# Squares for the first RMS sum added on VectorE instead of TensorE, and the first adaptive weights asked for one tile of x earlier

## The reference

```python
def rms_norm(x, g):
    xf = x.astype(jnp.float32)
    y = xf * lax.rsqrt(jnp.mean(xf * xf, axis=-1, keepdims=True) + EPS)
    return (y * g.astype(jnp.float32)).astype(x.dtype)
...
    cond = jax.nn.silu(c)
    for l in range(DEPTH):
        mod = cond @ w_ada[l] + b_ada[l]
        shift1, scale1, gate1, shift2, scale2, gate2 = [m[:, None, :] for m in jnp.split(mod, 6, axis=-1)]
        h = rms_norm(x, norm1_g[l]) * (1.0 + scale1) + shift1
        p_lru, p_sb, p_gdn, p_rw = _split(h @ w_in[l], MIXER_IN)
        ...  # four mixers, their gates and branches, w_out, a second norm, ConvFFN, a last norm
```

## Time and profile before

| | us |
|---|---|
| median of 3 runs | 1926.4 |
| the 3 runs | 1924.95 to 1929.25 |
| the profiled execution | 1924.12 |
| its span (first to last instruction) | 1922.3 |
| PE busy | 1873.8 (97%) |
| DVE busy | 935.1 |
| POOL busy | 919.5 |
| ACT busy | 456.5 |

### The profile page before, as it was taken

One profiled execution on the slowest core, in us unless ns is written; L12 is line 12 of the kernel. 1 busy time (PEld: TensorE's weight loads), 2 busy tenths in 40 slices (PEclk: granted clock), 3 DMA queues, 4 the chain that ended last, 5 costly groups with the idle time before them and its releaser, 6 DMA issues.

```text
span 1922.3 us, 33848 instructions
## 1 busy us (share of the span) xinstructions
PE 1873.8 (97%) x14266; PEld 1499.6 (78%) x14266; DVE 935.1 (49%) x1449; ACT 456.5 (24%) x715; POOL 919.5 (48%) x1100
## 2 busy tenths in 40 slices
PE   6999999999999999999999999999999999999997
PEld 4778777767787887887887787888888888888885
DVE  4856578754546546545545826432233322323326
ACT  4441344351222212213213413210110101101103
POOL 2777656523233223223324574455565555646655
PEclk9999999999999999999999999999999999999999
DMA  8516211232212122122135631111111111111112
GB/s 329 215 42 232 97 56 66 88 137 68 72 57 80 65 69 78 47 88 78 41 106 187 219 98 33 33 55 44 55 44 44 55 44 55 44 54 44 46 52 88
DMA packets 72025, 163.52 MB, mean 85 GB/s; under 512 B 6112, under 2 KB 30816, under 8 KB 71904
## 3 DMA queue, kind: packets, MB, share of 16 engines
q1 hardware_dynamic: 64416, 142.88, 22.2%
q10 hardware_dynamic: 7488, 18.88, 2.6%
HBM read 133.17 MB, written 28.57 MB: 84 GB/s over the span
## 4 chain that ended last, share of the span: by engine, by line
PE 83%; DVE 8%; issue 3%; POOL 2%; ACT 2%; DMA 1%; SPq 1%; DVEq 0%; ACTq 0%; POOLq 0%
PE gbank L639 55%; PE mbank L1215 11%; PE mbank L964 3%; PE gbank L1111 1%; POOL w_lo L533 1%; DVE state L2179 1%; DVE fa L1929 1%; POOL w_hi L529 1%; PE gbank L964 1%; PE mbank L720 1%; PE mbank L887 1%; PE gbank L741 1%; PE gbank L1170 1%; DVE fa L1856 1%; DVE h_lo L2308 1%
## 5 line engine op out<-in xcount | busy, mean ns | idle before, releaser
L529 POOL TENSOR_TENSOR w_hi<-w_raw,zero 128x256 fp32r<-128x256 f32 (+1 forms) x508 | 387.2, 792 | 930.9 <-PE gbank L639 767.6
L639 PE MATMUL gbank<-h_hi,w_hi 128*128 128x512 f32 x1648 | 657.7, 399 | 1.0 <-POOL w_lo L533 1.0
L639 PE MATMUL gbank<-h_lo,w_hi 128*128 128x512 f32 x1648 | 648.2, 393 | 0.0
L639 PE MATMUL gbank<-h_hi,w_lo 128*128 128x512 f32 x1648 | 647.9, 393 | 0.0
L533 POOL TENSOR_TENSOR w_lo<-w_raw,w_hi 128x256 fp32r<-128x256 f32 (+1 forms) x508 | 459.0, 934 | 10.0
L639 PEld LDWEIGHTS gbank<-h_hi,w_hi 128*128 128x128 f32 x1648 | 309.4, 188 | 79.1 <-issue 14.5
L639 PEld LDWEIGHTS gbank<-h_hi,w_lo 128*128 128x128 f32 x1648 | 309.4, 188 | 66.9 <-issue 1.5
L639 PEld LDWEIGHTS gbank<-h_lo,w_hi 128*128 128x128 f32 x1648 | 309.6, 188 | 65.4 <-issue 2.9
L1215 PE MATMUL mbank<-ra,w_hi 128*128 128x512 f32 x640 | 197.0, 389 | 0.0
L1215 PEld LDWEIGHTS mbank<-ra,w_hi 128*128 128x128 f32 x640 | 120.1, 188 | 24.9
L2355 DVE SCALAR_TENSOR_TENSOR fa<-mbank,mod,fa 128x1024 f32<-128x1024 f32 x40 | 51.4, 1284 | 169.2 <-PE mbank L1215 169.2
(11 more groups left out here) (355 smaller groups left out, 2196.7 us busy)
## 6 DMA issues: line engine op xcount, KB each, us to landing
w_raw<-in_w_tail SPq DMA_DIRECT2D x74, 512.0 KB, 3.7
fa<-in_w_ada SPq DMA_DIRECT2D x48, 512.0 KB, 6.0
w_raw<-in_w_in SPq DMA_DIRECT2D x26, 512.0 KB, 4.3
p_scr<-fa ACTq DMA_DIRECT2D x20, 512.0 KB, 2.7
w_raw<-in_w_mix SPq DMA_DIRECT2D x16, 640.0 KB, 4.0
fa<-in_xT SPq DMA_DIRECT2D x16, 512.0 KB, 7.9
w_raw<-in_w_gate SPq DMA_DIRECT2D x16, 512.0 KB, 4.0
sig_scr<-fa ACTq DMA_DIRECT2D x32, 256.0 KB, 2.0
```

Of the source, the lines that this page charges most:

```text
L529: last = pool.tensor_tensor(hi[:, c], raw[:, c], zero[:, 0:1].to_broadcast([P, w]), ALU.add)
L639: mm = pe.matmul(gb[bank], w, r, start=(q == 0), stop=(q == 3 * ks - 1))
```

## The change

Four edits belong together.

DVE adds the squares of x1 to x6 (six additions, not three). PE sums over features only the tile of those seven squares (`fa[:, 9]`) and that of x7 (`fa[:, 10]`): 4 multiplies, 8 instructions, not 20, and the first of them now waits for the sixth addition. `sq_used` counts the two finished halves. ACT's squares of x6 and x7 wait for DVE (`x_sq`) where they waited for PE, and its first logarithm waits for the first half alone. SP waits for x5, not for x6, before it asks for the adaptive weights.

```diff
@@ SP
-            sp.wait_ge(sem("x_in6"), 16)
+            sp.wait_ge(sem("x_in5"), 16)
             for t in range(16):
@@ PE
             pe.wait_ge(sem("ones_in"), 16)
-            for k in range(3, KT):
-                if k == 3:
-                    pe.wait_ge(sem("x_sq"), 3)
-                else:
-                    pe.wait_ge(sem("sq"), k + 1)
-                for hf in range(2):
-                    last = pe.matmul(mb[hf], m_("ones"), fa[:, 9 if k == 3 else 8 + 2 * (k % 2), hf * HALF:(hf + 1) * HALF],
-                                     start=(k == 3), stop=(k == KT - 1))
-                last.then_inc(sem("sq_used"), 1)
+
+            pe.wait_ge(sem("x_sq"), KT - 2)
+            for hf in range(2):
+                pe.matmul(mb[hf], m_("ones"), fa[:, 9, hf * HALF:(hf + 1) * HALF], start=True, stop=False)
+            pe.wait_ge(sem("sq"), KT)
+            for hf in range(2):
+                pe.matmul(mb[hf], m_("ones"), fa[:, 10, hf * HALF:(hf + 1) * HALF], start=False, stop=True).then_inc(sem("sq_used"), 1)
@@ ACT
             for k in range(KT):
                 act.wait_ge(sem(f"x_in{k}"), 16)
-                if 3 <= k < 6:
+                if k >= 3:
                     act.wait_ge(sem("x_sq"), k - 2)
-                elif k >= 6:
-                    act.wait_ge(sem("sq_used"), k - 4)
                 act.activation(fa[:, 8 + 2 * (k % 2) if k else 9, :], fa[:, k, :], ACT.Square).then_inc(sem("sq"), 1)
 
             act.preload_act_table_set("natural_log_exp_and_others")
-            act.wait_ge(sem("sq_used"), KT - 3)
             act.wait_ge(sem("zero_set"), 5)
             for hf in range(2):
+                act.wait_ge(sem("sq_used"), hf + 1)
                 act.activation(fa[:, 9, hf * HALF:(hf + 1) * HALF], mb[hf], ACT.Ln, bias=eps[:, 0:1],
                                scale=1.0 / D).then_inc(sem("ln1"), 1)
@@ DVE
-            for k in range(1, 4):
+            for k in range(1, KT - 1):
                 dve.wait_ge(sem("sq"), k + 1)
                 if k >= 2:
                     dve.wait_ge(sem("x_sq"), k - 1)
                 dve.tensor_tensor(fa[:, 9, :], fa[:, 9, :], fa[:, 8 + 2 * (k % 2), :], ALU.add).then_inc(sem("x_sq"), 1)
@@ DVE, mod_in
                 if part == 0:
-                    dve.wait_ge(sem("sq_used"), KT - 3)
+                    dve.wait_ge(sem("sq_used"), 2)
```

## The result

The changed kernel takes **1929.43 us** (median of 20 runs, 1927.66 to 1931.43) against 1926.39 for the kernel before, run on the same chips (20 runs, 1923.69 to 1929.64): ratio **1.0016**, 95% interval 1.001 to 1.0022. It is slower by 3.0 us, clear of the noise, but by less than the 0.2% that the prediction named as the line. The forecast was 1930.2, with a range of 1927.9 to 1932.3. One of the changed kernel's own executions was profiled; its span is 1928.4 us.

A forecast was written before the change was run, and what follows sets the result against it. PE is busy 97% of the span; at the start the later of transfer and norm paths binds. Norm path +4.2 us puts the first product 3.8 later: 1926.4 becomes 1930.2 us, range 1927.9 to 1932.3.

The forecast's parts named there:

- the 0.2%: Smallest difference from no change this kernel's measurement can tell, 3.9 us; the forecast 3.8 lies at that line.
- What bounds: At the start, transfer path (32.6 us, binding) and norm path (32.15) end within 0.5 us; the later sets PE's first product.
- The additions: DVE's additions and POOL's whole passes take turns: new ones about 3.2, 2.8 and 3.3 us, the sixth ending at 24.0.
- the first rival: DVE's additions do not wait for POOL's whole passes, ending at 19.4 to 19.7; faster by about 0.7, 1925.7 us; chance 0.07.
- The sum on PE: PE's eight sum instructions start cold at 24.15 us; the last starts at 28.9, 4.2 later than before.
- no rise in the sum: PE's clock stays low through all eight sum instructions: last start at 30.2, 5.5 us later than before.
- I take 4.2, the row of the same instructions: Choice for PE's sum: clock rises 3.3 us after the first multiply, as before; alternatives gave 3.8 and 5.5.
- What follows the sum: Part 0, h_norm and low part move along; the ask is hidden; first product at 36.4, 3.8 us later.
- The clock at the products: PE's first products begin at half clock, costing 1.3 us before; the forecast left this unchanged.
- the slow stretch: PE's clock at 0.51 between 31.8 and 35.2 us, 2.6 us of it on products, cost 1.3.
- the second rival: Clock stays full at the first products since part 1 is dense and later: −1.3, 1928.9 us; chance 0.27.
- The total: Whole kernel: +3.8 us on the median 1926.4 gives 1930.2; forecast's own chance 0.44.

The follow-up runs named there:

- ask_only: The kernel before with only the earlier ask (SP waits for x5, not x6): 1925.17 us, ratio to before 1.0001.
- pieces_late: The changed kernel with POOL's first split in pieces of 256 columns and SP's ask put back behind x6: 1925.8 us, ratio to before 1.0005.
- pieces: The changed kernel with POOL's first split in pieces of 256 columns instead of whole tiles of 1024: 1923.31 us, ratio to before 0.999.
- defer: The changed kernel with POOL's first split begun only after the sixth addition: 1924.41 us, ratio to before 0.9992.
- adds_only: The changed kernel with SP's ask put back behind x6, so only additions and sum differ from before: 1929.36 us, ratio to before 1.0024.
- warm: The changed kernel with 17 multiplies, results unread, keeping PE busy ahead of the sum: 1926.96 us, ratio to before 1.0012.
- before_pieces: The kernel before with only POOL's first split in pieces of 256 columns: 1925.32 us, ratio to before 1.0001.
- pieces_warm: The changed kernel with POOL's first split in pieces of 256 columns and 12 unread multiplies ahead of PE's sum: 1922.48 us, ratio to before 0.9984.

## Why the prediction came out right, point by point

**What bounds.** Right: two paths end close together in the kernel before, and the later one sets the first product. The distance was a little smaller than the 0.5 us of the prediction, since PE starts 0.14 us behind the end of the low part: ask_only, bound by the norm path, has the product 7.18 us behind the start of part 0, which in the kernel before would be 32.34, 0.3 before 32.61. In each run the first product follows the later of its two paths (in pieces_late both end together). What is lost or won at part 2 is found again in the medians, 1880 us later, to within 1.5 us.

**The additions.** Right, to 0.1 us in each of the three and in POOL's passes. The step that carried it was to read the durations of 1.54 and 3.21 in rows 4 not as slow instructions but as waits whose ends lie a fixed time behind the other engine's end (1.08 for DVE, 2.21 and 1.75 for POOL), and to see in rows 6 that the two take turns. The pieces run shows the mechanism by changing only the length of a turn. The Trainium skill, SBUF — State Buffer, section Who interferes with whom, calls the port pair that VectorE and GpSimd share an exclusive lock. These traces agree: what is waited for is a whole instruction, and an addition of 1.23 us takes 3.18. Additions that are not held up, as the first rival had them, are what defer has. Its median is 1.4 us below before with no change inside the interval, so whether that rival's 0.7 us would have been right is not shown.

**The sum on PE.** The mechanism was right and the size off. The last of eight instructions was to start 4.2 us later than before; from the square of x1 it is 30.84 − 9.04 = 21.8 against 24.64 − 8.13 = 16.5, **5.3 us**, close to the 5.5 that the prediction gave for no rise in the sum. The term that was off is "I take 4.2, the row of the same instructions": one measured distance from the first multiply to the rise of the clock (3.3 us) was taken for a property of the instructions. The other runs with this sum have from about 3.2 in pieces to about 6 in defer. From the start of the cold sum of eight to part 0 it is 5.17 us in pieces, 6.19 in pieces_late, 6.30 and 6.31 in the changed kernel and adds_only, and 6.64 in defer; warm it is 3.63 both times.

**What follows the sum.** Right: part 0, `h_norm` and the low part kept their distances, the ask was hidden, PE waited 2.48 us for the low part (forecast 2.4). The first product came at 29.5 from the square of x1 where 28.3 was forecast; of the 1.2 us, 1.1 are those of the sum (5.3 for 4.2) and 0.1 the step from the low part to PE.

**The clock at the products.** The forecast left the slow stretch as it was; the second rival took it away, and it is gone in the changed kernel. From the first product to part 2 it is 5.90 us instead of 7.07. That gave 1.2 us back and hid the error of the sum: at part 2 the changed kernel stands 35.40 − 31.55 = 3.85 us behind, forecast 3.8. Two errors of one size and opposite sign; the good agreement is partly luck. The rival's reason, a dense and later part 1, is not borne out. Warm has the same dense part 1 and the same idle 2.48 us behind it, and its products begin at half clock (7.48 us to part 2); before_pieces has part 1 in three portions with waits between, as before, and its products run at full clock (5.89). Four of the ten profiled executions have the slow stretch (before, ask_only, warm, pieces_warm). What decides it stays open.

**The total.** The medians say 3.0 and the two profiled starts 3.85. The profiled spans differ by 6.1: 0.9 of it is the late landing of x, and about 1.5 the slow stretch near 420 us. Five of the ten profiles have a stretch at half clock there, between 413 and 423 us: the changed kernel, adds_only, defer, pieces_late and before_pieces. The last has the old additions and the old sum, so the stretch does not need the change; but both kernels that make the additions beside whole passes and leave the sum cold have it, and two of the three with the old sum do not. Whether the change makes it more frequent, one profile of each does not tell. If it does, the change costs more than the start shows, not less, so it does not explain why the medians say 3.0 and not 3.85. That stays open.

## What to carry to other kernels

When an elementwise instruction of VectorE with two inputs in SBUF is put beside GpSimd's work, price it by the whole GpSimd instruction it may have to wait for, not by the slowdown seen where the two overlapped for a moment; and cut GpSimd's instructions short where VectorE's are on the path. Before moving work off TensorE at a cold start, ask what clock the rest will run at: twelve instructions of twenty were removed here and the sum of eight, started 9.4 us later, cost 6.3 us instead of 10.4. A transfer asked for earlier gives nothing while the path beside it is later (adds_only against the changed kernel), so test such edits together and apart. And before a gain or loss of 1 us is put down to an edit, look at what the clock did in the same execution: here it moved single stretches by 1.2 to 1.5 us on its own.

## What the runs showed of the hardware that was not expected

- The time from PE's first multiply to its full clock is not fixed: the sum of eight, the same instructions on an idle engine, took from 5.17 to 6.64 us to the next step in five executions, and the sum of twenty from 10.4 to 11.7 in three.
- At the start of a program the clock column of the profile shows 1.00 (21.0 to 30.5 us in the changed kernel) while weight loads take 0.34 us instead of 0.19. At a start the durations are to be read, not the column.
- A slow stretch of TensorE's clock can come far from a change: five of ten profiles have one near 420 us, and in the changed kernel it cost about 1.5 us, half of what the whole change made. Whether the first products run at half clock did not follow from how dense the work ahead of them was.
- The first tiles of x landed up to 2.2 us apart from one profiled execution to another (square of x1 at 7.09 to 9.29), with the same asks in front. The 20 runs of the kernel before span 6 us and those of the changed kernel 3.8, so this can be a good part of the scatter of a single run; how large a part was not measured.
